# Layer norms whose squares are summed on VectorE before one product over the partitions

## The reference

```
def layer_norm(x, g, b):
    mu = jnp.mean(xf, -1, keepdims=True)
    var = jnp.mean(jnp.square(xf - mu), -1, keepdims=True)
    return ((xf - mu) * lax.rsqrt(var + LN_EPS) * g + b).astype(x.dtype)
...
        x = layer_norm(ALPHA * x + mix, ln1_g[l], ln1_b[l])
        hdn = jnp.square(jax.nn.relu(x @ ffn_w1[l]))
        x = layer_norm(ALPHA * x + hdn @ ffn_w2[l], ln2_g[l], ln2_b[l])
        e = rms_norm(p[l] @ ple_w_proj[l], ple_norm_g[l])
        x = x + jax.nn.sigmoid(x @ ple_w_gate[l]) * e
```

## Time and profile before

| | |
|---|---|
| median of three runs | 1994.88 us |
| profiled execution | 1999.76 us |
| its span, first to last instruction | 1998.5 us |
| mean granted TensorE clock | 0.978 |
| centring to reciprocal root, norm 1 | 217.16 to 230.08 us |
| norm 2 | 431.22 to 448.28 us |
| norm 3 | 653.73 to 664.50 us |
| norm 4 | 860.10 to 870.56 us |

### The profile page before, as it was taken

One profiled execution on the slowest core, in us unless ns is written; L12 is line 12 of the kernel. 1 busy time (PEld: TensorE's weight loads), 2 busy tenths in 40 slices (PEclk: granted clock), 3 DMA queues, 4 the chain that ended last, 5 costly groups with the idle time before them and its releaser, 6 DMA issues.

```text
span 1998.5 us, 35689 instructions
## 1 busy us (share of the span) xinstructions
PE 1905.6 (95%) x14792; PEld 1721.6 (86%) x14792; DVE 1273.6 (64%) x2327; ACT 980.6 (49%) x1732; POOL 77.3 (4%) x78
## 2 busy tenths in 40 slices
PE   5998999989999999999999999999999998989997
PEld 4775798989888999988798878999999987679997
DVE  3535664668777856576777555665666776656665
ACT  3454443556555645466645443544445653434443
POOL 0000100002000200020010010000000000100000
PEclk9999999999999999999999999999999998889999
DMA  8788867655533465645144433555565443125664
GB/s 305 259 292 308 280 198 247 182 156 164 156 92 113 154 188 180 191 137 165 59 145 133 143 97 120 165 182 188 190 190 175 132 128 110 27 85 175 185 183 123
DMA packets 93825, 334.92 MB, mean 168 GB/s; under 512 B 10960, under 2 KB 12880, under 8 KB 93536
## 3 DMA queue, kind: packets, MB, share of 16 engines
q1 hardware_dynamic: 92016, 327.33, 51.9%
q0 software_dynamic: 1648, 5.31, 0.9%
HBM read 331.55 MB, written 1.05 MB: 166 GB/s over the span
## 4 chain that ended last, share of the span: by engine, by line
PE 89%; DMA 4%; DVE 4%; ACT 2%; issue 1%; SPq 1%; DVEq 0%
PE bank L548 23%; PE bank L550 22%; PE bank L549 22%; PE bank L823 4%; PE bank L790 4%; DMA ring_side<-in_stream 2%; PE bank L677 2%; PE bank L587 2%; PE bank L805 2%; DMA ring_mod<-in_stream 2%; PE bank L589 2%; PE bank L588 2%; PE bank L1104 1%; PE bank L965 1%; PE bank L1797 1%
## 5 line engine op out<-in xcount | busy, mean ns | idle before, releaser
L523 DVE TENSOR_TENSOR low<-ring,high 128x1024 fp32r<-128x1024 f32 x410 | 501.9, 1225 | 261.7 <-ACT high L515 260.7
L548 PE MATMUL bank<-XHx,high 128*128 128x256 f32 x2096 | 611.2, 292 | 31.5 <-DVE XLx L629 22.1
L549 PE MATMUL bank<-XLx,high 128*128 128x256 f32 x2096 | 596.8, 285 | 0.0
L550 PE MATMUL bank<-XHx,low 128*128 128x256 f32 x2096 | 596.5, 285 | 0.0
L515 ACT CAST high<-ring 128x1024 fp32r<-128x1024 f32 x410 | 428.0, 1044 | 333.2 <-PE bank L550 291.1
L548 PEld LDWEIGHTS bank<-XHx,high 128*128 128x128 f32 x2096 | 404.5, 193 | 55.4 <-issue 38.5
L549 PEld LDWEIGHTS bank<-XLx,high 128*128 128x128 f32 x2096 | 405.5, 193 | 0.9
L550 PEld LDWEIGHTS bank<-XHx,low 128*128 128x128 f32 x2096 | 405.3, 193 | 0.0
L548 PE MATMUL bank<-XHc,high_side 128*128 128x256 f32 x608 | 180.6, 297 | 11.4 <-DVE low_side L523 10.1
L523 DVE TENSOR_TENSOR low_side<-ring_side,high_side 128x1024 fp32r<-128x1024 f32 x110 | 134.7, 1224 | 71.5 <-ACT high_side L515 70.9
L550 PE MATMUL bank<-XHc,low_side 128*128 128x256 f32 x608 | 172.3, 283 | 0.0
(11 more groups left out here) (432 smaller groups left out, 3179.4 us busy)
## 6 DMA issues: line engine op xcount, KB each, us to landing
ring<-in_stream SPq DMA_DIRECT2D x410, 512.0 KB, 3.7
ring_side<-in_stream SPq DMA_DIRECT2D x110, 512.0 KB, 3.7
ring_mod<-in_stream SPq DMA_DIRECT2D x96, 512.0 KB, 5.1
x_nb<-in_rpb POOLq DMA_DIRECT2D x12, 256.0 KB, 3.1
Xx<-in_x SPq DMA_DIRECT2D x2, 512.0 KB, 4.7
Xc<-in_ctx SPq DMA_DIRECT2D x1, 1024.0 KB, 7.7
out<-y SPq DMA_DIRECT2D x8, 128.0 KB, 2.0
pT<-in_p POOLq DMA_DIRECT2D x2, 256.0 KB, 4.6
```

Source lines behind the costliest of these rows:

```text
L523: nc.vector.tensor_tensor(st.low[:, j % st.n_ring, :], st.ring[:, j % st.n_ring, :], st.high[:, j % st.n_split, :].bitcast(F32), ALU.subtr ...
L548: nc.tensor.matmul(out, wh, xh, start=(i == 0), stop=False)
L549: nc.tensor.matmul(out, wh, xl, start=False, stop=False)
L550: m = nc.tensor.matmul(out, wl, xh, start=False, stop=(c == ks[-1]))
```

## The change

In the four layer norms the squares are summed over the 8 parts on VectorE, and one product sums over the partitions. The first square is written straight into `RS` (its contents, the sum for the mean, have been read by then), the other seven go into `SQ` as before, and VectorE adds each to `RS` behind the centrings. A buffer of `SQ` is freed by its addition. The product with `meanD` is made once, on `RS`, and its PSUM bank is taken behind the last addition instead of at the first square. `tensor_squares` stays for the first norms of the second block.

```diff
@@ -1091,7 +1091,17 @@
     T.wait_ge(k.s_vec, (yield tag, "total"))
     nc.tensor.matmul(k.bank[b][:, 0:SEQ], k.c["meanD"][:, :], w.RS[:, 0, 0:SEQ], start=True, stop=True).then_inc(
         *T.tick(k.s_sums, T_us(SEQ, 4), (tag, "mean")))
-    yield from tensor_squares(k, w, tag)
+    yield from tensor_square_total(k, w, tag)
+
+
+def tensor_square_total(k, w, tag):
+
+    nc, T = k.nc, k.T
+    T.wait_ge(k.s_vec, (yield tag, "squares", DC - 1))
+    b = yield from w.banks.take(T, (tag, "log"))
+    k.bank_of[tag, "squares"] = b
+    nc.tensor.matmul(k.bank[b][:, 0:SEQ], k.c["meanD"][:, :], w.RS[:, 0, 0:SEQ], start=True, stop=True).then_inc(
+        *T.tick(k.s_sums, T_us(SEQ, 4), (tag, "summed", DC - 1)))
 
 
 def tensor_squares(k, w, tag):
@@ -1110,9 +1120,13 @@
     nc, A = k.nc, k.A
     for i in range(DC):
         A.wait_ge(k.s_x_done, (yield tag, "centred", i // 2))
-        j = k.sq_of[tag, i] = yield from w.sq.take(A, (tag, "summed", i))
-        nc.scalar.activation(w.SQ[:, j, 0:SEQ], w.X[:, i, :], ACT.Square).then_inc(
-            *A.tick(k.s_squares, A_us(SEQ), (tag, "square", i)))
+        if i == 0:
+
+            out = w.RS[:, 0, 0:SEQ]
+        else:
+            j = k.sq_of[tag, i] = yield from w.sq.take(A, (tag, "squares", i))
+            out = w.SQ[:, j, 0:SEQ]
+        nc.scalar.activation(out, w.X[:, i, :], ACT.Square).then_inc(*A.tick(k.s_squares, A_us(SEQ), (tag, "square", i)))
     A.wait_ge(k.s_sums, (yield tag, "summed", DC - 1))
     yield from rstd(k, k.bank[k.bank_of[tag, "squares"]][:, 0:SEQ], w.RS[:, 0, 0:SEQ], 0, (tag, "log"), (tag, "rstd"))
     for i in range(DC):
@@ -1130,6 +1144,14 @@
         nc.vector.tensor_tensor(xs, xs, mean, ALU.subtract).then_inc(
             *V.tick(k.s_x_done, V_us(2 * SEQ), (tag, "centred", i)))
         yield None
+    rs = w.RS[:, 0, 0:SEQ]
+    for i in range(1, DC):
+        V.wait_ge(k.s_squares, (yield tag, "square", i))
+        if i >= 2:
+            V.wait_ge(k.s_vec, total)
+        nc.vector.tensor_tensor(rs, rs, w.SQ[:, k.sq_of[tag, i], 0:SEQ], ALU.add).then_inc(
+            *V.tick(k.s_vec, V_us(SEQ), (tag, "squares", i)))
+        total = V.last
     for step in range(DC + 2):
         if step < DC:
             x = w.X[:, step, :]
```

## The result

The change makes the kernel slower. The median is 2006.44 us (2000.89 to 2018.12, 9 runs) against 1993.76 us (1990.02 to 1999.22, 9 runs) on the same chip: a ratio of 1.0059, with a 95% interval of 1.0042 to 1.0076, some 12 us. The forecast was 1986.2 us, and its range ended at 1998.5.

The account below looks back on a forecast made before the run. TensorE's work was taken to bound the kernel while products are ready, otherwise a chain of waits. Norm gains 3.0 + 3.0 + 1.2 + 1.5 = 8.7 us off 1999.76 gave 1991.1, with factor 0.9976 1986.2 us; range 1977 to 1998.5.

Parts of the forecast that it names:

- The order, priced at 0: Everything after the changed costs: new instruction order, one longest side-tile split wait more or less, +-4.4 us, taken as 0.
- 28 x 0.43 = 12.0 us: TensorE, four norms: 28 squares' products removed at 0.43 us each, 12.0 us of work.
- Rival (a): Removed TensorE work becomes idle time, up 8 us or more; only the third norm's 1.2 us won; 1993.7 us, chance 0.19.
- The chain has slack in every norm: Each norm: bare chain 7.6 us, against 12.92, 17.06, 10.77 and 10.46 us, even with 2 us of VectorE's other work.
- rival (b): VectorE: additions queue behind context splits awaiting DMA, 4.4 us; each norm loses 2.3 us; 2004.1 us, chance 0.12.
- First: First norm: chain shortens by 4 to 5 us, less moved modulation tiles; 3.0 us won.
- Second: Second norm: the 3.75 us stall before the first square stays; 3.0 us won.
- Third: Third norm: 3.0 us of work removed, less a 1.8 us wait of the single product; 1.2 us won.
- Fourth: Fourth norm: chain falls from 10.46 to some 9 us; 1.5 us won, with ends 0 and 3.0.
- rival (c): Third and fourth norm: granted clock falls without the squares' products, 7.4 us lost; 1993.6 us, chance 0.06.
- The factor and the range: Whole kernel: 0.9976 converts profiled 1999.76 us to the runs' median 1994.88; range 1977 to 1998.5 us.
- the difference lies after 912 us: then it is the new order: Failure test: a difference after 912 us, where none of the changed code runs, would show the new order.

Follow-up runs that it names:

- the nudged kernel: Kernel before, same instructions, 0.3 us added to TensorE's modelled clock at the second norm's centring, so what follows is ordered anew: 2007.68 us, 1.0058.
- two of the reordered kernels: Both ordered anew by the program: changed kernel with the third norm's eight products kept, 1.0009; kernel before with only the third norm summed on VectorE, 0.9998.
- the additions in place: The change in the kernel before's recorded order, each addition where its product stood, single product where the eighth stood: 2003.18 us, 1.0036; again 2004.39 us, 1.0026.
- that norm alone: Kernel before, its order held, additions only in the norm under discussion: first norm 1998.55 us, 1.001; third norm 2002.16 us, 1.0033.
- the embedding modelled late: Changed kernel, with the embedding's transfer modelled to land 8 us after issue instead of 3: 2008.07 us, 1.0071.
- The third norm alone: Kernel before, its order held, additions in the third norm only, each where its product had stood: 2002.16 us, 1.0033.
- The same norm alone in an order of the program's own: Kernel before with only the third norm summed on VectorE, ordered anew by the program: 1995.0 us, 0.9998.

## Why the prediction was wrong

**The order, priced at 0.** The prediction named it as "one part no row prices", gave it +-4.4 us and took 0 "with no reason for either sign". Four nudged or re-costed orders of the old instructions lost 8 to 12 us, and none won. This is the step that failed most: alone it makes the whole measured 12 us. The waits behind it were the right kind, for a side tile's split, but the nudged kernel has one more of them and 6.6 us more in all, not 4.4, and TensorE idles for 13.6 us more in all. There may have been a reason for the sign, too. A TensorE that is busy for 10.46 of 10.46 us beside a chain of waits shows that work and waits fit, and a random move will rather disturb that. This is an inference and not shown: two of the reordered kernels lost nothing.

**"28 x 0.43 = 12.0 us" won.** The price was near: the net fall was 13.9 us. Its worth was not. With the additions gone altogether, and no square waiting for a buffer, 3.8 us are won. In the fourth norm the single product then waits for ScalarE's last square:

```profile
867.22 0.70 PE L1103 MATMUL bank<-RSx,c_meanD 128*128 128x256 f32 x2 [2.50 <-ACT SQx L1129]
```

The products had filled time that the squares took anyway. Rival (a), the work turns into idle time, was right about these 28 products, and the sign it expected, idle time up by 8 us or more, is there with 10.7. Its time, 1993.7 us, was wrong all the same: it had to say what else is added.

**"The chain has slack in every norm."** The bare chain was 7.6 us, with seven additions back to back in 3.2. VectorE's timeline of the additions in place, fourth norm, shows what they met:

```profile
871.49 0.43 DVE L1152 TENSOR_TENSOR RSx<-RSx,SQx 128x256 f32<-128x256 f32 x1 [0.57 <-ACT SQx L1129]
872.43 1.23 DVE L523 TENSOR_TENSOR low<-ring,high 128x1024 fp32r<-128x1024 f32 x1 [0.51 <-ACT high L515]
873.57 0.42 DVE L1316 TENSOR_TENSOR RSx<-RSx,SQx 128x256 f32<-128x256 f32 x1
873.91 0.99 DVE L1152 TENSOR_TENSOR RSx<-RSx,SQx 128x256 f32<-128x256 f32 x2
875.41 1.23 DVE L523 TENSOR_TENSOR low_side<-ring_side,high_side 128x1024 fp32r<-128x1024 f32 x1 [0.51 <-ACT high_side L515]
876.55 2.00 DVE L1152 TENSOR_TENSOR RSx<-RSx,SQx 128x256 f32<-128x256 f32 x4
```

And ScalarE in the same stretch:

```profile
871.04 0.42 ACT L1129 ACTIVATE SQx<-Xx 128x256 f32<-128x256 f32 x1 [1.23 <-DVE RSx L1316]
...
874.02 0.42 ACT L1129 ACTIVATE SQx<-Xx 128x256 f32<-128x256 f32 x1 [1.00 <-DVE RSx L1316]
```

The seven additions take from 871.49 to 878.55, 7.1 us instead of 3.2. Two splits of 1.23 us stand between them, with their waits for the casts. Two buffers hold the squares of the norm and of the embedding, and now VectorE's additions free all of them. So ScalarE waits for VectorE and VectorE for ScalarE in turn. Room on an engine, as I read it from busy time, is not room at the place in its queue. This is rival (b)'s mechanism in half: the additions do queue among the splits. But those splits wait for casts, 0.51 us each, not for a DMA of 4.4. It gave 2004.1 us, and the additions in place, where the order is held, took 2003.18. That the two agree is luck, since the price was made of other waits. Casts that wait for a tile's transfer, as (b) has it, do stand in the norms, but they are shorter: 1.07 us in the fourth norm of the kernel after, 1.79 in the second of the additions in place, 2.86 in the third with the embedding modelled late.

**Norm by norm.** *First:* the chain got shorter, 12.92 to 10.96 us with the additions in place, but with that norm alone nothing was won (1.001). The modulation tiles' transfers seem to set the pace: in its profile TensorE waits 2.54, 0.94 and 0.80 us for them, in before 0.54, 1.33 and 0.35. *Second:* 3.0 us were forecast, and the chain changed from 17.06 to 17.63 us. The stall ahead of the first square (3.75 us in the earlier trace rows) is gone and a longer one stands elsewhere: 5.10 us for the embedding's copy, line 1287, then 3.43 for the context's normed part, line 1651. *Third:* the wait of the single product was 0.90 us where I took 1.8, and 1.71 with that norm alone, so that term was not too cheap. (Its source was misread: the 11.0 us in 6 places of the earlier trace rows count the weight loads and the products of the same waits. TensorE's own are 5.2 us in 3 places, which gives 1.7.) The others, 0.59, 0.92 and 1.31 us for the context's recurrence on ScalarE and VectorE, I had not counted. *Fourth:* I counted no wait and 1.5 us won; the single product waits 4.64 us there, and the chain grew from 10.46 to 12.67.

**The clock, rival (c).** TensorE in the third norm, a stretch of 4.10 us (view of windows, clock third from the end). The additions in place:

```profile
668.40:672.50 4.10, 4.10 (x21) 3.98 (x21) 1.70 (x4) 2.17 (x3) 0.00 (x0) 0.50 0.00 0
```

Before:

```profile
668.40:672.50 4.10, 4.10 (x35) 4.00 (x35) 4.10 (x8) 3.82 (x7) 4.10 (x5) 1.00 0.26 51
```

It is busy all the time in both, at 1.2 GHz in the one and 2.4 in the other, with 21 records against 35. The clock fell behind two rests of 0.59 and 0.92 us, and was low when the other two waits of this norm came:

```profile
659.30:662.40 3.10, 1.59 (x16) 1.34 (x16) 3.04 (x9) 2.04 (x7) 0.00 (x0) 1.00 0.57 160
662.60:668.40 5.80, 3.58 (x22) 2.13 (x20) 4.29 (x11) 2.61 (x5) 0.00 (x0) 0.50 0.01 4
```

So behind short waits the same work takes longer. The Trainium skill, "TensorE: Matmul & The Clock Gate", Part 1, has the low clock as the default that activity lifts; the trace agrees here. What part of the loss is the clock's is not shown. The third norm alone loses 0.33% (0.19 to 0.46), 6.6 us, with 4.7 us of waits in the norm. The same norm alone in an order of the program's own has 5.0 us of waits and a longer stretch of low clock, and loses nothing. I gave (c) 0.06 and as a thing apart from (b), but here it came with the waits; in the kernel after it came in the third norm (0.62) and not in the fourth (1.00).

**The factor and the range.** 1999.76 and 0.9976 held well enough: before was 1993.76 again. The range's high end took one bad order at +4.4 us. With what the runs show it had to reach 2008. My test "the difference lies after 912 us: then it is the new order" was no test: in after the third mean starts 0.76 us earlier than in before and the fourth 8.23 us later, so by this profile the loss falls ahead of 912 us, though the order is its cause. In the nudged kernel most of it falls behind: its fourth mean starts at 862.46 us, 3.39 later than before's, and its last product of line 1694 at 1998.06, 8.50 later. A small slip besides: (b)'s 0.12 and the 0.02 of (a) and (c) make slower 0.14, not 0.13, and same 0.22. The mean's product in the third and fourth norm on TensorE's timeline, after:

```profile
651.57 0.67 PE L1092 MATMUL bank<-RSx,c_meanD 128*128 128x256 f32 x2
...
867.30 0.59 PE L1092 MATMUL bank<-RSx,c_meanD 128*128 128x256 f32 x2
```

And before:

```profile
652.33 0.59 PE L1092 MATMUL bank<-RSx,c_meanD 128*128 128x256 f32 x2
...
859.07 0.60 PE L1092 MATMUL bank<-RSx,c_meanD 128*128 128x256 f32 x2
```

## What to carry to other kernels

Where a program orders its instructions by modelled times, a change is two changes: hold the recorded order to see what the edit is worth, and nudge the old kernel to see what an order is worth; here the second was 8 to 12 us and the first 5 to 7, both against the edit, and they do not add up. In a chain with fill around it, read what the chain waits for at each step before counting work taken off the busiest engine: some 14 us of TensorE were worth 3.8. And look where an added instruction lands in its queue, and which buffers now come free there, not at the share of time that the engine is idle.

## What the runs showed of the hardware that was not expected

How much a rest costs after its end. In the fourth norm of the additions in place TensorE's fill, behind the single product that had waited 4.64 us, ran at half its clock for 4.9 us though it was busy in all but 0.01 of them:

```profile
878.60:883.50 4.90, 4.89 (x21) 4.71 (x22) 2.68 (x7) 3.51 (x10) 0.91 (x1) 0.50 0.00 0
```

So 2.5 us of TensorE's work were lost in the 4.9, on top of the wait. This differs from one execution to the next. The second profile of the same kernel has the same wait of 4.64 us in front of the product at 873.03 us, and behind it the low clock lasts for 3.2 us:

```profile
873.03:876.20 3.17, 3.17 (x13) 2.99 (x14) 0.96 (x3) 1.86 (x6) 0.00 (x0) 0.50 0.00 0
```

In the third norm two rests of 0.59 and 0.92 us stood in front of a low clock. The additions were longer than I took them from end to end: 2 in 0.95 or 0.99 us, 4 in 2.00, with 0.42 us for the last one. That is 0.53 us from one start to the next where I had 0.45, some 2 us more over 28.
